# The softmax division moved from the probabilities to the head outputs, with the SyncE queue and GpSimd's order rearranged around it

## What is computed

```
def _attend(q, k, v, cum_q, cum_kT, q_pos):
    s = jnp.einsum("bqhd,bkhd->bhqk", q, k).astype(jnp.float32) * ATTN_SCALE
    s = s + jnp.swapaxes(cum_q, 1, 2)[..., None] - cum_kT[:, :, None, :]
    ...
    p = jax.nn.softmax(s, axis=-1).astype(v.dtype)
    return jnp.einsum("bhqk,bkhd->bqhd", p, v)
```

## Time and profile before

| | us |
|---|---|
| median of 3 runs (2902.79 to 2909.69) | 2908.66 |
| the profiled execution, its own time | 2906.83 |
| its span in the trace | 2905.2 |
| PE busy | 2696.3 |
| DVE busy | 1109.6 |
| POOL busy | 951.4 |
| ACT busy | 784.1 |

### The profile page before, as it was taken

One profiled execution on the slowest core, in us unless ns is written; L12 is line 12 of the kernel. 1 busy time (PEld: TensorE's weight loads), 2 busy tenths in 40 slices (PEclk: granted clock), 3 DMA queues, 4 the chain that ended last, 5 costly groups with the idle time before them and its releaser, 6 DMA issues.

```text
span 2905.2 us, 44679 instructions
## 1 busy us (share of the span) xinstructions
PE 2696.3 (93%) x16907; PEld 2605.1 (90%) x16907; DVE 1109.6 (38%) x2082; ACT 784.1 (27%) x1431; POOL 951.4 (33%) x546
## 2 busy tenths in 40 slices
PE   8999969999999999689997899889799999999994
PEld 8999959999999999579996778779599999999993
DVE  3222362422222222762354555552642222222237
ACT  2111134111111111252223555551511111111114
POOL 2212143112111122352323878843512212112114
PEclk9999969999999999899998989989899999999997
DMA  3111101111111111024688555631011111111111
GB/s 111 44 51 43 45 22 37 47 49 44 45 44 44 53 50 44 23 80 144 197 286 270 143 168 152 179 111 44 22 44 52 44 52 45 44 52 45 44 37 59
DMA packets 203054, 225.87 MB, mean 78 GB/s; under 512 B 13223, under 2 KB 168871, under 8 KB 201884
## 3 DMA queue, kind: packets, MB, share of 16 engines
q1 hardware_dynamic: 194748, 190.40, 21.5%
q0 software_dynamic: 8160, 33.30, 3.7%
HBM read 182.43 MB, written 41.26 MB: 77 GB/s over the span
## 4 chain that ended last, share of the span: by engine, by line
PE 79%; DVE 7%; POOL 4%; issue 4%; DMA 3%; ACT 2%; SPq 1%; POOLq 0%; DVEq 0%; ACTq 0%
PE ps L1746 24%; PE ps L1747 24%; PE ps L1748 24%; POOL ss L830 2%; PE ps L2012 2%; DVE ln_t L1405 1%; DVE ln_t L1409 1%; PE ps L2042 1%; DVE ln_d L1350 1%; PE ps L1997 1%; PE ps L1994 1%; DMA ncb<-ccum 1%; DMA o_t<-oe 1%; PE ps L2029 1%; PE ps L2028 1%
## 5 line engine op out<-in xcount | busy, mean ns | idle before, releaser
L1746 PE MATMUL ps<-xh,whi 128*128 128x344 f32 x3288 | 1068.0, 325 | 31.5 <-POOL xl L711 18.4
L1747 PE MATMUL ps<-xl,whi 128*128 128x344 f32 x3288 | 1055.2, 321 | 0.0
L1748 PE MATMUL ps<-xh,wlo 128*128 128x344 f32 x3288 | 1055.0, 321 | 0.0
L664 POOL TENSOR_TENSOR wlo<-wraw,whi 128x1024 fp32r<-128x1024 f32 x197 | 471.2, 2397 | 1659.0 <-ACT whi L890 1658.9
L1746 PEld LDWEIGHTS ps<-xh,whi 128*128 128x128 f32 x3288 | 620.7, 189 | 59.5 <-POOL xl L711 34.6
L1748 PEld LDWEIGHTS ps<-xh,wlo 128*128 128x128 f32 x3288 | 622.3, 189 | 0.0
L1747 PEld LDWEIGHTS ps<-xl,whi 128*128 128x128 f32 x3288 | 622.1, 189 | 0.0
L890 ACT ACTIVATE whi<-wraw 128x1024 fp32r<-128x1024 f32 x197 | 208.2, 1058 | 1116.9 <-DMA wraw<-ffn_w_gu 649.3
L1746 PE MATMUL ps<-zh,whi 128*128 128x344 f32 x1440 | 465.7, 323 | 17.6 <-DVE x L1477 9.4
L1747 PE MATMUL ps<-zl,whi 128*128 128x344 f32 x1440 | 464.1, 322 | 0.0
L1748 PE MATMUL ps<-zh,wlo 128*128 128x344 f32 x1440 | 462.1, 321 | 0.0
(11 more groups left out here) (209 smaller groups left out, 2384.3 us busy)
## 6 DMA issues: line engine op xcount, KB each, us to landing
wraw<-ffn_w_gu SPq DMA_DIRECT2D x88, 512.0 KB, 3.9
wraw<-ffn_w_down SPq DMA_DIRECT2D x44, 512.0 KB, 3.5
kp<-cache_k SPq DMA_DIRECT2D x32, 512.0 KB, 5.5
vp<-cache_v SPq DMA_DIRECT2D x32, 512.0 KB, 4.1
wraw<-a_w_in SPq DMA_DIRECT2D x24, 512.0 KB, 3.7
wraw<-kv_w SPq DMA_DIRECT2D x16, 512.0 KB, 4.3
q_t<-hl POOLq DMA_DIRECT2D x8, 1024.0 KB, 4.6
v_t<-vst POOLq DMA_DIRECT2D x8, 1024.0 KB, 6.9
```

The source lines that it names most:

```text
L664: pool.tensor_tensor(narrow(wlo[:, s, :], cols), narrow(wraw[:, s, :], cols), f32(narrow(whi[:, s, :], cols)), ALU.subtract).then_inc(w_lo, 1)
L1746: pe.matmul(out, w_h, m_h, start=start, stop=False)
L1747: pe.matmul(out, w_h, m_l, start=False, stop=False)
L1748: return pe.matmul(out, w_l, m_h, start=False, stop=stop)
```

## The change

The probabilities go to PE undivided. The eight reciprocals of a head are taken by one instruction per head in place of four, into `ri[:, e]`, which SP stores to a new DRAM row `r_t` (`store_sums`: 128 partitions with 8 values each, 4 bytes per piece, since a partition holds every 128th row). The row is read back, broadcast over the partitions, into `rb[e]` (`load_sums`), and POOL multiplies the whole output of the head by it (`scale`) before the halves are stored. For the last pair both rows go to `rlast`, and DVE multiplies `ost` once. The lists of SP and POOL are written in a new order.

```
-        rs = ma.put("rs", [P, STEPS, 2], F32)
-        ri = ma.put("ri", [P, STEPS, 2], F32)
+        rs = ma.put("rs", [P, 2, STEPS, 2], F32)
+        ri = ma.put("ri", [P, 2, STEPS, 2], F32)
...
+        rb = [Area(PAGES_AT - 3 * D * 4 + e * TP * 4).put(f"rb{e}", [P, TP], F32) for e in range(2)]
+        rlast = Area(XH_AT + 5 * TP * 4).put("rlast", [P, TP], F32)
...
+        r_t = nc.dram_tensor("r_t", [H, TP], F32, kind="Internal").ap()
...
+            sp.wait_ge(kv["s3dma"], 16 * 2)
+
+            def store_sums(b, e):
+
+                inverted = sp.to_reg(2 * b + e + 1 + 2) if not isinstance(b, int) else 2 * b + e + 1 + 2
+                apart(sp)
+                sp.wait_ge(at["rinv"], inverted)
+                sp.dma_start(r_t[bass.ds(2 * b + e, 1), :].rearrange("a (n p) -> p (a n)", p=P),
+                             ri[:, e, :, :].rearrange("p j t -> p (j t)"), allow_slow_non_contiguous=True).then_inc(r_st[e], 16)
+
+            def load_sums(b, e):
+
+                stored_sums = sp.to_reg(16 * (b + 2)) if not isinstance(b, int) else 16 * (b + 2)
+                apart(sp)
+                sp.wait_ge(r_st[e], stored_sums)
+                sp.dma_start(rb[e][:, :], r_t[bass.ds(2 * b + e, 1), :].to_broadcast([P, TP])).then_inc(r_in[e], 16)
 
             def store_head(b, e):
 
+                scaled = sp.to_reg(2 * b + e + 1)
                 apart(sp)
-                sp.wait_ge(at["odone"], PAIR * b + STEPS * (e + 1) + 2)
+                sp.wait_ge(at["omul"], scaled)
                 sp.dma_start(o_t[bass.ds(b, 1), e * DH:(e + 1) * DH, :].rearrange("a p t -> (a p) t"),
                              oe[e][0:DH, :]).then_inc(oe_st[e], 16)
 
@@ -583,20 +605,40 @@
                 sp.wait_ge(at["ofull"], summed)
                 load_v(b + 1, e)
 
-            with sp.Fori(0, KB - 1) as b:
-                next_qk(b, 0)
+            def pair(b, last=False):
+
                 load_v_page(b, 2)
+                next_qk(b, 1)
                 load_v_page(b, 3)
-                next_qk(b, 1)
                 next_v(b, 0)
+                store_sums(b, 1)
                 store_head(b, 0)
+                load_sums(b, 1)
                 load_v_page(b + 1, 0)
                 load_v_page(b + 1, 1)
                 next_v(b, 1)
+                if not last:
+                    next_qk(b + 1, 0)
+                store_sums(b + 1, 0)
                 store_head(b, 1)
+                if not last:
+                    load_sums(b + 1, 0)
+
+            next_qk(0, 0)
+            store_sums(0, 0)
+            load_sums(0, 0)
+            with sp.Fori(0, KB - 2) as b:
+                pair(b)
+            pair(KB - 2, True)
 
             load_v_page(KB - 1, 2)
             load_v_page(KB - 1, 3)
+            store_sums(KB - 1, 1)
+            sp.wait_ge(at["ofull"], PAIR * (KB - 1) + STEPS)
+            for e in range(2):
+                sp.wait_ge(r_st[e], 16 * (KB + 1))
+                sp.dma_start(rlast[e * DH:(e + 1) * DH, :],
+                             r_t[2 * KB - 2 + e:2 * KB - 1 + e, :].to_broadcast([DH, TP])).then_inc(r_in[0], 16)
...
-            def norm(b, st):
-
-                j = st % STEPS
-                inverted = pool.to_reg(PAIR * b + st + 1) if not isinstance(b, int) else PAIR * b + st + 1
+            def scale(b, e):
+
+                summed = pool.to_reg(PAIR * b + STEPS * (e + 1) + 2)
                 apart(pool)
-                pool.wait_ge(at["rinv"], inverted)
-                for t in range(2):
-                    pool.tensor_scalar(ss[j][:, t, 0:span(st, t)], ss[j][:, t, 0:span(st, t)], ri[:, j, t:t + 1], None,
-                                       ALU.mult).then_inc(at["pnorm"], 1)
+                pool.wait_ge(at["odone"], summed)
+                loaded = pool.to_reg(16 * (b + 1))
+                apart(pool)
+                pool.wait_ge(r_in[e], loaded)
+                pool.tensor_tensor(oe[e][:, :], oe[e][:, :], rb[e][:, :], ALU.mult).then_inc(at["omul"], 1)
...
             k_split(0, 0)
             store_ktok(KB - 1, 0)
             store_ktok(KB - 1, 1)
-            norm(0, 0)
             sample_rows_out()
             k_split(0, 1)
-            for st in range(1, STEPS):
-                norm(0, st)
             for m in range(WR):
                 low(SLOTS["o"] + m, SLOTS["o"] + m)
-            with pool.Fori(0, KB - 1) as b:
-                norm(b, STEPS)
-                k_split(b + 1, 0)
-                for st in range(STEPS + 1, PAIR):
-                    norm(b, st)
+            def pair(b, last=False):
+
+                k_split(b + 1, 1)
+                scale(b, 0)
                 add_halves(b, 0)
-                norm(b, PAIR)
-                k_split(b + 1, 1)
-                for st in range(PAIR + 1, PAIR + STEPS):
-                    norm(b, st)
+                if not last:
+                    k_split(b + 2, 0)
+                scale(b, 1)
                 add_halves(b, 1)
-            for st in range(STEPS, PAIR):
-                norm(KB - 1, st)
+
+            k_split(1, 0)
+            with pool.Fori(0, KB - 2) as b:
+                pair(b)
+            pair(KB - 2, True)
...
+                e = st // STEPS % 2
+                if j == 0 and t == 0:
+
+                    act.wait_ge(at["rinv"], 2 * (b + st // PAIR) + e + 1)
                 act.activation(ss[j][:, t, 0:span(st, t)], ss[j][:, t, 0:span(st, t)], ACT.Exp, bias=nm[:, j, t:t + 1], scale=-1.0,
-                               accum_out=rs[:, j, t:t + 1]).then_inc(at["exp"], 1)
+                               accum_out=rs[:, e, j, t:t + 1]).then_inc(at["exp"], 1)
...
-            act.wait_ge(at["odone"], 2 + PAIR * KB)
+            act.wait_ge(at["onorm"], 1)
...
             def inverse(b, st):
-                j = st % STEPS
-                dve.wait_ge(at["exp"], 2 * (PAIR * b + st) + 2)
-                dve.reciprocal(ri[:, j, :], rs[:, j, :]).then_inc(at["rinv"], 1)
+
+                e = st // STEPS % 2
+                stored_sums = dve.to_reg(16 * (b + st // PAIR + 1)) if not isinstance(b, int) else 16 * (b + st // PAIR + 1)
+                apart(dve)
+                dve.wait_ge(r_st[e], stored_sums)
+                summed = dve.to_reg(2 * (PAIR * b + st) + 2) if not isinstance(b, int) else 2 * (PAIR * b + st) + 2
+                apart(dve)
+                dve.wait_ge(at["exp"], summed)
+                dve.reciprocal(ri[:, e, :, :], rs[:, e, :, :]).then_inc(at["rinv"], 1)
...
-                if not (last and st + 2 >= PAIR):
+                if (st + 2) % STEPS == STEPS - 1 and not (last and st + 2 >= PAIR):
                     inverse(b, st + 2)
...
-            for st in range(2):
                 step(0, st)
...
-                if m == 5:
+                if m == 3:
                     dve.wait_ge(at["odone"], 2 + PAIR * KB)
+                    dve.wait_ge(r_in[0], 16 * (KB + 1))
+                    dve.tensor_tensor(ost[:, :], ost[:, :], rlast[:, :], ALU.mult).then_inc(at["onorm"], 1)
...
-                    pe.wait_ge(at["pnorm"], 2 * s + 2)
+                    pe.wait_ge(at["exp"], 2 * s + 2)
```

More of the change, by code:

```diff
@@ L339, in build @@
         at = {k: sem(f"at_{k}") for k in
-              ("khi", "klo", "sfull", "sdr", "exp", "rinv", "pnorm", "tfull", "pthi", "ptlo", "ofull", "ohalf", "odone")}
+              ("khi", "klo", "sfull", "sdr", "exp", "rinv", "omul", "onorm", "tfull", "pthi", "ptlo", "ofull", "ohalf", "odone")}
         oe_st = [sem(f"oe_st{e}") for e in range(2)]
         oe_add = [sem(f"oe_add{e}") for e in range(2)]
+        r_st = [sem(f"r_st{e}") for e in range(2)]
+        r_in = [sem(f"r_in{e}") for e in range(2)]
         sm = {k: sem(f"sm_{k}") for k in
@@ L552, in load_v_page @@
                 page = sp.value_load(pt[0:1, bass.ds(b * PPB + g, 1)], min_val=0, max_val=a["cache_v"].shape[0] - 1)
-                used = sp.to_reg(PPB * b + g + 1)
+                used = sp.to_reg(PPB * b + g + 1) if not isinstance(b, int) else PPB * b + g + 1
                 apart(sp)
@@ L1272, in _ @@
             for n, (s, credit) in enumerate(((ffn[0]["sum"], DBANKS), (ffn[0]["down"], 1), (at["ptlo"], 2), (at["odone"], 2),
+                                             (at["rinv"], 2), (r_st[0], 16), (r_st[1], 16),
                                              (kv["vt"], 2), (kv["vtok"], 2), (kv["vl"], 2),
@@ L1696, in _ @@
                     maxima(0, st, t)
-            for st in range(2):
-                inverse(0, st)
             for st in range(2):
```

## The result

The changed kernel is slower: 2938.38 us (median of 4 runs, 2932.80 to 2942.50) against 2907.89 us of before (4 runs), ratio 1.0106, interval 1.0084 to 1.0129. The prediction was 2880 us with a range of 2862 to 2897, and gave "slower" 0.06. The profiled execution took 2932.8 us, its span is 2931.1 us.

The account below looks back on a forecast made before the run. POOL, multiplying probabilities, was taken to bound the attention stage by PE's waits and slowed clock. Gains 23.4 (heads) + 6.5 (start) + 0 - 1.0 = 28.9 us: 2877.9 from the profiled 2906.8, forecast 2880 us, range 2862 to 2897.

Parts of the forecast that it names:

- the round trip of the sums: Reciprocals stored to DRAM and read back: store taken at 7.8 us, read-back 6.2 us, 11 us left over, cost nothing.
- rival D: Slower than before: store and accumulating DMA land so late that ACT waits; 4-byte pieces blocking DMA rings; 2971 us, chance 0.05.
- The sentence on the Trainium skill: Warning about the small-piece store of the sums; if it doubled the 2.7 us landing, the sum would not move.
- the new chain to the release of `oe`: Loads, key split, scaling, store and accumulating DMA end at +26.9 us, ACT overwrites at +26.7; cost nothing, cover 2 us.
- Rival C: `oe` released late: three landings each 1.7 us over their median, 21 us of the gain gone, 2901 us, chance 0.07.
- SyncE's queue: Loads behind `load_sums` and `store_head`: pages and values needed more than 8 us after issue, so cost nothing.
- `norm` and the clock: Attention heads: without POOL's multiplications and with most of PE's clock back, a head falls from 21.9 to 20.1 us.
- the bound: Best possible attention head at full clock, all parts set by ACT and PE: 8.7 + 4.97 + 5.96 = 19.6 us.
- in a minority of heads: Where PE's clock was still expected to fall, costing 0.5 us per head on average.
- start: Start of the attention stage: PE's waits for POOL shrink or go, 3.5 + 0.5 + 2.5 = 6.5 us gained.
- heads: Thirteen heads from the second head to the last pair, 21.9 to 20.1 us each: 23.4 us gained.
- the end of the stage with what follows: Last pair zero net, 2.4 us of `scale` against norm waits; last product with `rlast` behind the stage, -1.0 us.

Follow-up runs that it names:

- f: d with the 4-byte store of the reciprocals put back on SyncE at its changed-kernel places, nobody reading the row: 2930.38 us, ratio 1.0081 to the kernel before.
- d: Changed kernel with neither store nor load of the reciprocals; POOL multiplies by ones, output not divided: 2895.35 us, ratio 0.9952 to the kernel before.
- j: a with reciprocals taken by VectorE and stored by SyncE in 1024 pieces of 4 bytes into DRAM, nobody reading them: 2931.76 us, ratio 1.0082.
- a: Kernel before with the multiplication of the probabilities and the reciprocals left out, nothing in their place, output not divided: 2870.09 us, ratio 0.9861.
- k: f with the store in 128 pieces of 32 bytes in place of 1024 of 4: 2898.24 us, ratio 0.9960 to the kernel before.
- n: j with the store in 128 pieces of 32 bytes into the same DRAM row: ratio 0.9867 to the kernel before.
- m: j with the same 1024 pieces of 4 bytes written into SBUF and not into DRAM: ratio 0.9864 to the kernel before.
- e: d with POOL's order changed so that it scales ahead of the key split: 2874.11 us, ratio 0.9890 to the kernel before.
- c: Changed kernel with the store in 128 pieces of 32 bytes, row read back in the wrong order: 2909.10 us, ratio 1.0010 to the kernel before.
- i: Changed kernel, whole computation, with 32-byte store pieces, strided products, and POOL scaling ahead of the key split: 2876.74 us, ratio 0.9885 to the kernel before.
- b: Changed kernel with one exchange, POOL scaling a head before it splits the next keys: 2927.00 us, ratio 1.0068 to the kernel before.
- l: j with the store in 512 pieces of 8 bytes in place of 1024 of 4: ratio 0.9906 to the kernel before.
- g: Changed kernel with store and load of the sums on GpSimd's queue, scaling ahead of the key split: 2967.26 us, ratio 1.0210 to the kernel before.

## Why the prediction was wrong

**The step that failed first** is *the round trip of the sums*: "both ends cost nothing: 11 us are left". I bounded the store's own landing (0 to 7.8 us, "three times" the 2.7 us of a DMA of 64-byte pieces, which would be 8.1) and asked only who waits for it. It landed after 14.2 us, above the bound, but that is the smaller fault. The cost that counts is borne by transfers that nobody had connected with it: 1.3% in f over d, 2.2% in j over a, with nobody reading the row. The words that its pieces could hold up other transfers stand in rival D, at 0.05, with the objection that "little but the first half stands directly behind it". Two things in that were wrong: transfers issued just ahead of the store suffer too (`ncb` in f, issued 0.77 us ahead of `r_t`, 17.7 us for the 10.8 of d), and in the changed kernel's lists the loads of `next_qk`, on which the split keys hang, stand right there. In the changed kernel itself the chain shown at 1684.95 is no proof of it: its `ncb` took 11.7 us, within the 7.6 to 12.0 of such heads in k.

The sentence on the Trainium skill (DMA: Bandwidth & Descriptors, Specifications and Rules for kernel authors) said: one descriptor per element for a strided last dimension, and a read-modify-write below 512 bytes. On the first the traces agree for SyncE's queue (j's page has 211388 packets in the queue of SyncE, that of before 194748: 16640 more, 16 stores of 1024 pieces and 16 others each). By the second, j and n should both have suffered, and n didn't, while m shows that the count alone does no harm. How the memory handles such a write no run here shows. I had taken the warning as one about the transfer's own time; here most of the cost fell on its neighbours, of which that sentence says nothing.

**The second** is *the new chain to the release of `oe`*, costed "at nothing, with a cover of just 2 us". It did not hold. Without any trip (d) the chain overran it and ACT waited 48.0 us in 11 waits; d against e prices `scale` behind the key split at 0.6%, some 18 us. With the trip in 32-byte pieces it is worth 1.25% (c against i, whose product is also the strided one). Rival C had the mechanism, with 21 us, at 0.07. The term that was mis-sized is the landings, taken from the medians of the earlier trace rows: in d `ncb` took 7.9 us for 6.2 and the accumulating DMA 7.2 for 4.6, with no more bytes than before; in e, with the same list of SyncE and another order of POOL, 6.3 and 4.1.

**SyncE's queue**, costed at nothing: its stores waited 176.3 us for POOL in the changed kernel, and PE 21.7 us for pages issued behind them. In i no such wait of PE for pages is left, so this was a consequence, not a cost of its own.

**Right, and shown by a and i:** `norm` and the clock. a's heads take 19.65 us, i's 19.8, against 20.1 forecast and 19.6 as the bound. In i ten of the thirteen heads take 19.3 to 19.7 us (most of them less than the 19.6 called the bound) and three 21.2, with a stretch at PEclk 0.57 in one of the latter: the clock does fall "in a minority of heads". What makes it fall in those and not in others no run here tests. The sum of i, in the terms of the prediction: start 6.1 us (6.5; 1616.76 - 1610.66), heads 284.84 - 257.67 = 27.2 (23.4), and the end of the stage with what follows 29.3 - 6.1 - 27.2 = -4.0 (-1.0), where 29.3 is the difference of the spans, 2905.2 - 2875.9; forecast 28.9. Within the -4.0, the last product takes 2.0 us, being strided, and the wait of `ost` for the last accumulating DMA is 7.3 us, 1.0 over the earlier trace rows; the rest was not traced further. i at 2876.7 us is what the prediction of 2880 described; the kernel as changed lacked two conditions that I had counted as met.

**Between the two kernels** the 30.5 us (2938.4 - 2907.9) are thus: -1.4% for `norm` (a), +0.3% for what e adds to it (the product on POOL and the new lists), +0.6% for the place of `scale` (d over e), +1.3% for the store's effect on others (f over d), and +0.25% for reading the row back and waiting (the changed kernel over f). These add up in this order only; the parts overlap, as b, c and i show, and the two of 0.3% and 0.25% are not clear of the noise.

## What to carry to other kernels

The transposing store here, 4 KB into DRAM, was priced by its pieces and by what else was in flight, not by its bytes or its reader: let each partition write its values side by side and undo the order with a stride on the reading engine, which cost 0.6 us of an idle GpSimd here. A cover of 2 us on a chain of 27 us with three landings in it is no cover, since landings taken from another order of issue don't hold in the new one: put the step that the chain needs ahead of the one that waits for a transfer. And where a resource has no row in the trace, bound what it does to the neighbours as well as its own duration.

## What the runs showed of the hardware

- 1024 writes of 4 bytes into DRAM by one DMA brought the core's transfers down to 25 to 70 GB/s for some 10 us, from 282 GB/s just before (j); 512 of 8 bytes to 80 GB/s for about 4 us (l). Behind 128 of 32 bytes the same 4 us had 183 GB/s (n), behind 1024 of 4 bytes into SBUF 175 (m); these landed in 2.4 and 2.7 us and cost nothing.
- The stall reaches a transfer issued 0.77 us earlier: in f it landed 17.7 us after its issue, some 6 us of them with no packet in the profile; without the store it took 10.8 us (d). Behind such a store on GpSimd's queue SyncE's loads moved at 36 to 75 GB/s (g).
- A DMA's median landing depends on what is issued beside it, with the same bytes in all: the accumulating DMA took 7.2 us in d and 4.1 us in e, which differ in GpSimd's order alone.
- GpSimd's product of 128x1024 float32 takes 2.37 us with both inputs contiguous and 3.00 us with one read in steps of 32 bytes; VectorE's 1.23 and 2.02 us.
